# A two-layer decoder trunk: every matrix product with tokens as output rows and 512 weight columns moving, the FFN in two parts, state chunks of 8 tokens, and a program without loops

## What is computed

```python
for i in range(2):
    h = rms_norm(x, norm_mix[i])
    x = x + (gmlp_mixer(h) if i == 0 else s5_mixer(h))
    h = rms_norm(x, norm_ffn[i])
    x = x + (silu(h @ w1[i]) * (h @ w3[i])) @ w2[i]                 # 2048 -> 5632 -> 2048
    gate = sigmoid(rms_norm(x, norm_ple[i]) @ ple_w_gate[i])        # 2048 -> 2048
    x = x + gate * (p[i] @ ple_w_proj[i])                           # 256 -> 2048
return rms_norm(x, norm_final)

# gmlp_mixer: z = gelu(h @ w_in), u, v = split(z); v = layer_norm(v)
#             (u * (tril(w_s) @ v + b_s)) @ w_out, per chunk of 128 tokens and head of 128
# s5_mixer:   u = h @ w_in; 128 groups of 16 channels, 64 complex states each:
#             s[t] = lam_bar * s[t-1] + b_bar @ u[t];  y = Re(c @ s) + d * u
#             val, gate = split(gelu(y) @ w_out);  val * sigmoid(gate)
```

## Time and profile before

| | |
|---|---|
| median of 3 runs | 2567.61 us (2559.71 to 2567.79) |
| span of the profiled execution | 2571.7 us |
| PE busy, and matmul records | 2447.3 us (95%), 14304 |
| DVE, ACT, POOL busy | 1651.7, 1154.5, 329.0 us |
| mean granted clock of PE | 0.971 |
| DMA, mean | 188 GB/s |

### The profile page before, as it was taken

How to read it: one execution, slowest core, us unless ns; L and a number is a source line. 1 busy time by engine, 2 the same in 40 slices (tenths; PEclk the granted TensorE clock), 3 DMA queues, 4 the chain that set the end, 5 groups by cost and what they waited for, 6 DMA issues and landing times.

```text
span 2571.7 us, 39073 instructions
## 1 busy us (share of the span) xinstructions
PE 2447.3 (95%) x14304; PEld 2136.3 (83%) x14304; DVE 1651.7 (64%) x1758; ACT 1154.5 (45%) x1224; POOL 329.0 (13%) x363
## 2 busy tenths in 40 slices
PE   7999798999999999999999999999999999999996
PEld 5887587778878888888889988888888888888885
DVE  7765977767876655555766765666565565555565
ACT  5544244444444444444632224555545555444453
POOL 2001725545552000000000000000000000000000
PEclk9999899999999999999999889999999999999998
DMA  7654376666776665555577865566666666655652
GB/s 239 190 161 134 106 244 194 197 206 181 203 219 205 181 192 188 184 185 177 190 246 218 240 197 165 184 190 184 183 181 194 182 186 186 187 185 185 187 173 99
DMA packets 301371, 484.04 MB, mean 188 GB/s; under 512 B 58800, under 2 KB 85568, under 8 KB 301024
## 3 DMA queue, kind: packets, MB, share of 16 engines
q1 hardware_dynamic: 300224, 479.01, 61.1%
q0 software_dynamic: 848, 3.74, 0.4%
q10 hardware_dynamic: 208, 0.07, 0.0%
HBM read 453.65 MB, written 29.10 MB: 188 GB/s over the span
## 4 chain that ended last, share of the span: by engine, by line
PE 77%; DVE 8%; issue 6%; POOL 5%; ACT 2%; DMA 2%; DVEq 0%; SPq 0%; ACTq 0%; POOLq 0%
PE PS L1570 42%; PE PS L1571 21%; DVE WLO L1052 2%; PE PS L1590 2%; PE PS L1591 2%; PE PS L1592 2%; PE PS L1788 1%; PE PS L1772 1%; PE PS L1663 1%; PE PS L1664 1%; PE PS L1665 1%; PE PS L1786 1%; POOL DTB L703 1%; DMA RAW<-in_s_w_in 1%; POOL DT L704 1%
## 5 line engine op out<-in xcount | busy, mean ns | idle before, releaser
L1052 DVE TENSOR_TENSOR WLO<-RAW,WHI 128x1024 fp32r<-128x1024 f32 x788 | 987.2, 1264 | 822.6 <-ACT WHI L758 818.7
L758 ACT ACTIVATE WHI<-RAW 128x1024 fp32r<-128x1024 f32 x788 | 829.2, 1058 | 1024.6 <-PE PS L1571 871.7
L1570 PE MATMUL PS<-H,WHI 128*128 128x512 f32 x3328 | 1184.1, 401 | 17.4 <-DVE WLO L1052 14.6
L1571 PE MATMUL PS<-H,WLO 128*128 128x256 f32 x3328 | 937.7, 282 | 0.0
L1570 PE MATMUL PS<-M,WHI 128*128 128x512 f32 x2304 | 824.0, 402 | 23.3 <-DVE WLO L1052 21.5
L1570 PEld LDWEIGHTS PS<-H,WHI 128*128 128x128 f32 x3328 | 628.8, 189 | 179.0 <-DVE WLO L1052 21.8
L1571 PE MATMUL PS<-M,WLO 128*128 128x256 f32 x2304 | 652.0, 283 | 0.0
L1571 PEld LDWEIGHTS PS<-H,WLO 128*128 128x128 f32 x3328 | 632.8, 190 | 0.0
L1570 PEld LDWEIGHTS PS<-M,WHI 128*128 128x128 f32 x2304 | 438.0, 190 | 134.3 <-issue 26.7
L1571 PEld LDWEIGHTS PS<-M,WLO 128*128 128x128 f32 x2304 | 440.9, 191 | 0.0
L648 POOL PARTITION_ALL_REDUCE SUM<-SS x7 | 16.1, 2296 | 1585.7 <-DVE SS L1084 1566.8
(11 more groups left out here) (225 smaller groups left out, 1805.9 us busy)
## 6 DMA issues: line engine op xcount, KB each, us to landing
RAW<-in_ffn_w SPq DMA_DIRECT2D x528, 512.0 KB, 3.9
RAW<-in_gm_w_in SPq DMA_DIRECT2D x64, 512.0 KB, 4.1
RAW<-in_ple_w_gate SPq DMA_DIRECT2D x64, 512.0 KB, 4.3
RAW<-in_s_w_out SPq DMA_DIRECT2D x64, 512.0 KB, 4.0
RAW<-in_gm_w_out SPq DMA_DIRECT2D x32, 512.0 KB, 4.1
RAW<-in_s_w_in SPq DMA_DIRECT2D x32, 512.0 KB, 5.3
tabd<-DT SPq DMA_DIRECT2D x16, 512.0 KB, 6.1
tabq<-QS SPq DMA_DIRECT2D x16, 512.0 KB, 4.8
```

Source lines behind the costliest of these rows:

```text
L758: A_.activation(WHI[:, slot, :], RAW[:, slot, :], ACT.Copy).then_inc(hi_ready, 1)
L1052: V_.tensor_tensor(WLO[:, slot, :], RAW[:, slot, :], WHI[:, slot, :].bitcast(F32), ALU.subtract).then_inc(lo_ready, 1)
L1570: T_.matmul(PS[:, QB * s + m, :], WHI[:, slot, w], operand(k), start=(k == 0), stop=False)
L1571: last = T_.matmul(PS[:, QB * s + m, TOK:2 * TOK], WLO[:, slot, w], operand(k)[:, 0:TOK], start=False, stop=(k == TK * depth - 1))
```

## The change

- Every product uses the form of `v`: stationary are 128 tokens by 128 features of the operand, 512 weight columns move, 12 matmuls a tile in one function `tile`. `X` is kept token-major. There are 792 tiles still.
- The next operand must be feature-major, so each finished quarter (4 blocks of 128 features, a quad) is transposed by PE (`turn`, 8 transposes), one or two tiles after the column that made it; ACT and DVE then split it straight out of PSUM (`high`, `low`). There are 50 quads, 4 of them for the input.
- RMS statistics are `bn_stats` along a row on DVE; the reciprocal root is a number for each partition and goes into the activation's scale. `partition_all_reduce`, `cross`, `total` and `scaled` go.
- The FFN runs in two parts (6 and 5 pairs of columns), with the down product of each part after it, so that its operand needs less room.
- S5 chunks are of `T` = 8 tokens, `NC` = 32 chunks. POOL builds all tables, per block: `QT` and `DT` of 512 elements a partition in 12 operations. PE turns `QT` (8 transposes) at `BUILD_A[b]` and makes the taps (9 matmuls) three tiles later, at `BUILD_B[b]`. Tables are kept per group of 16 channels. POOL also makes the rotation tables alone and two of the layer norm's steps.
- The state stage covers 32 tiles of `win` and 24 of `out1` (`EARLY`). Per duo `into_states` has 32 matmuls with 64 stationary columns and 32 moving; `out_of_states` has 16 with 128 by 128 stationary and 32 with 64 rows. u is turned feature-major again (`turn_u`) before it goes through DRAM.
- All hardware loops are written out.

```diff
-STAGES = [
-    ("pro", 1, dict(a=5, q=8, r=4)),
...
+STAGES = [("v", NT, 8), ("us", NT, 8), ("out0", NT, 8),
+          ("up0a", 2 * FA, 8), ("dn0a", NT, 2 * FA), ("up0b", 2 * FB, 8), ("dn0b", NT, 2 * FB), ("gate0", NT, 9),
+          ("win", NT, 8), ("out1", 2 * NT, 8),
+          ("up1a", 2 * FA, 8), ("dn1a", NT, 2 * FA), ("up1b", 2 * FB, 8), ("dn1b", NT, 2 * FB), ("gate1", NT, 9)]
...
+INTO_AT = [W0 + 8 * (d // 2) + 15 + d % 2 for d in range(DUOS)]
+OUT_AT = [W0 + 8 * (d // 2) + 18 + 2 * (d % 2) for d in range(DUOS)]
...
+            def tile(t, dst, block_, first, last_one):
+                slot = t % RING
+                pe.wait_ge(lo_ready, t + 1)
+                for kk in range(TK):
+                    f = slice(NW * kk, NW * kk + NW)
+                    for th in range(2):
+                        hi = OP_of(block_ + kk)[:, P * th:P * th + P]
+                        lo = OP_of(block_ + kk)[:, TOK + P * th:TOK + P * th + P]
+                        begin, finish = first and kk == 0, last_one and kk == TK - 1
+                        T_.matmul(dst[:, th, :], hi, WHI[:, slot, f], start=begin, stop=False)
+                        T_.matmul(dst[:, th, :], hi, WLO[:, slot, f], start=False, stop=False)
+                        last = T_.matmul(dst[:, th, :], lo, WHI[:, slot, f], start=False, stop=finish)
+                last.then_inc(split_used, 1)
...
+                for m in range(QB):
+                    for th in range(2):
+                        src = Z[:, th, P * m:P * m + P] if row is None else X[:, th, NW * i + P * m:NW * i + P * m + P]
+                        at = TOK * (m % 2) + P * th
+                        last = T_.transpose(PS[:, bank + m // 2, at:at + P], src, IDENT[:, :])
...
+            def spread_u(n, h):
+                sp.wait_ge(ud_in, 16 * (n + 1))
...
+                if b:
+                    pool.wait_ge(taps_done, b)
+                    pool.wait_ge(d_out, 16 * b)
```

More of the change, by code:

```diff
@@ L65 @@
 QP = 4
+GB = 8
 DUOS = KB // 2
-STAGES = [
-    ("pro", 1, dict(a=5, q=8, r=4)),
[L73 to L92, removed]
@@ new lines, with start, end, odd_up @@
+ORDER = plan()
+TILES = len(ORDER)
+INDEX = {key: t for t, key in enumerate(ORDER)}
+DEPTH_OF = {name: depth for name, _, depth in STAGES}
+def start(stage, n=0):
+    return INDEX[stage, n, 0]
+def end(stage, n):
+    return INDEX[stage, n, DEPTH_OF[stage] - 1] + 1
+def odd_up(stage, n):
+    return stage[:2] == "up" and n % 2 == 1
+def taken_by_dve(stage, n):
+    return stage[:2] in ("dn",) or stage == "out0" or odd_up(stage, n)
+COLUMNS = sorted(((end(s, n), s, n) for s, cols, _ in STAGES for n in range(cols)))
@@ new lines, with quads @@
+TURN_OF = {key: c for c, key in OWNER.items()}
+QUADS = [("x", n, n, 4 * n, 0, None, 4 + 2 * (n % 2)) for n in range(NT)]
+def quads(stage, cols, block, row, after, per=1):
+    for i, n in enumerate(cols):
+        QUADS.append((stage, n, i, block + 4 * i, row, end(stage, n) + after, 4))
+quads("us", range(NT), 16, None, 1)
+quads("out0", range(NT), 0, 2, 1)
+quads("up0a", range(1, 2 * FA, 2), 16, None, 1)
+quads("up0b", range(1, 2 * FB, 2), 16, None, 1)
+quads("dn0b", range(NT), 0, 4, 1)
+quads("gate0", range(NT), 24, 1, 2)
@@ new lines @@
+RMS = {"v": 0, "us": 0, "up0a": 1, "up0b": 1, "gate0": 2, "win": 3, "up1a": 4, "up1b": 4, "gate1": 5}
+BUILD_A = [start("up0a", 2 * b) + 9 for b in range(FA)] + [start("dn0a", n) + 5 for n in range(NT)]
+BUILD_A += [start("up0b", 2 * b) + 9 for b in range(FB)] + [start("dn0b") + 5]
+BUILD_B = [t + 3 for t in BUILD_A]
+CT_AT = [start("out0") + 12 + 4 * r for r in range(4)]
+MIX_AT = [start("us", n) + 6 for n in range(NT)]
+SET_AT = start("v", 1)
+WT_AT = [start("v", 2) + 2, start("v", 2) + 6]
+PT1_AT = start("up1a") + 5
@@ new lines, in ups @@
+            def ups(stage, pairs, first_block=None):
+                for i in range(pairs):
+                    if i:
+                        quad_of(stage, i - 1, 1)
+                    until(end(stage, 2 * i))
+                    take(stage, 2 * i, in_s, ACT.Silu)
+                    if first_block is not None:
+                        tables(first_block + i)
+                    if stage == "up1a" and i == 0:
+                        until(PT1_AT + 1)
+                quad_of(stage, pairs - 1, 1)
@@ new lines, in downs, with gates @@
+            def downs(stage, i):
+                for n in range(NT):
+                    quad_of(stage, n, 1)
+                until(end(stage, NT - 1) + 4)
+                root(i)
+            def gates(stage, i, last=True):
+                for n in range(NT):
+                    until(end(stage, n))
+                    take(stage, n, in_s, ACT.Sigmoid)
+                    if last:
+                        quad_of(stage, n, 2)
+                if last:
+                    until(end(stage, NT - 1) + 5)
+                    root(i)
@@ new lines, in gates @@
+            def gates(stage, i):
+                for n in range(NT):
+                    until(end(stage, n))
+                    gated(stage, n, PS[:, 6:8, :])
+                    quad_of(stage, n, 2)
+                moments()
+                until(end(stage, NT - 1) + 7)
+                reciprocal(i)
+            ups("up0a", FA)
+            for n in range(NT):
+                add_acc("dn0a", n)
+            ups("up0b", FB)
+            residuals("dn0b", 2)
+            gates("gate0", 3)
```

2260 lines of the change are left out of this document (1051 added, 1209 removed).

## The result

The changed kernel takes 2497.23 us (median of 4 runs, 2493.33 to 2500.09) beside 2567.7 us of the kernel before (4 runs). The ratio is 0.9723, with a 95% interval of [0.969, 0.9755]: 2.8% faster, where 2431 us, 5.3%, was forecast. Direction and time lie inside what was given as a whole (2375 to 2515), but the time lies outside the range of the forecast proper (2385 to 2475); 66 us of the forecast gain are missing.

The account below looks back on a forecast made before the run. PE bounds the kernel. Tiles at 2154 us plus start, turns, tables, state stage, other stages' extras and end sum to a 2435 us span, median 2431, 5.3% less; range 2375 to 2515, the forecast's own 2385 to 2475.

Parts of the forecast that it names:

- The rate: All 792 tiles: 2.72 us each as in `v`, some 15 ns a matmul beside the columns, 2154 us in all.
- A turn: Eight transposes on PE, 0.87 us, plus 0.10 at restart: 0.97 us each, 48.5 us for 50.
- The tables and their turns: Up and down stages with tables: 32 us of PE work for 16 blocks, 5 us of waits for POOL, plus turns.
- Rival C: Stages with tables: POOL late with each block at 3.2 us an operation, 60 us more, 2490 us; chance 0.07.
- Rival E: Whole unrolled program: instruction fetch stalls PE, 145 us at every sixth tile, 2650 at every fourth; chance 0.08.
- list of gains by stages: Gains: 70 and 11 us from rate, 50 tables, 26 `out0`, 7 `us`, 9 start and end; transposes cost 48.5, state stage 4.
- I take 30 us, bounds 10 and 90: State stage: waits and half clock together, beside tiles and small matmuls, put at 30 us.
- Rival B: State stage: DRAM data late, SP's waits holding weight loads, 58 us more waits, some 30 of clock, 2520 us; chance 0.15.
- The prediction's own sign: Wrong if PE waits at turns for DVE, taps for POOL, or states for a DMA over 60 us in all.
- the small matmuls: State stage: matmuls into and out of states, 12.5 us a duo, 100 us in all, bounds 67 and 142.
- `v`: Stage `v`: 12 us beyond its tiles, bounds 6 and 20; the stall on DVE goes, input turns and weight transposes stay.
- `us`: Stage `us`: beyond its tiles 2 us of waits and 10.4 for mixes, 16.3 with 4 turns.

Follow-up runs that it names:

- the last version: Changed kernel with y's DMAs from GpSimd, four bursts, duo 5's y wanted later, start reordered, layer norm's gain and bias on DVE: 2405.53 us, ratio 0.9321.

## Why the prediction was right and where it failed

**Right.** The rate: 2.72 us a tile, in every stage that has nothing else, so some 15 ns beside the columns of each matmul holds for the FFN's tiles as it did for those of `v`. A turn is 0.80 + 0.12 = 0.93 us where 0.97 was taken. The tables and their turns cost 44.9 us for 51.5: 31 of PE's work for 32, and nothing of the 5 us of waits, since POOL is never late. Rival C had POOL's operations too long: the twelve of 512 elements take 1.1 to 2.2 us each, 18.2 a block, where it had 3.2 each and 38. Rival E did not come: 29151 written-out instructions feed PE without a gap in 620 us of FFN. The end is 14.8 us for 17. DVE stays at half in the FFN, 309.55 of 619.8 us, as said. Its list of gains by stages, though, doesn't add up to its own sum: 70 + 11 + 50 + 26 + 7 + 9 less 48.5 and 4 is 121 us of the 137, and the rest was put to `v` and the gates without a figure.

**The step that failed** is "I take 30 us, bounds 10 and 90" for waits and half clock in the state stage. It was 188.6 less 4 turns (3.7) and 76 to 78 of small matmuls, some 107 us, beyond the upper bound. Rival B, at 0.15, named the mechanism: data through DRAM late on an SP queue whose waits hold the weight loads, and the clock falling with the gaps. Its 88 us of waits and 30 of clock, 118, are near the 107, but divided otherwise: 48 idle, 59 of clock. The prediction gave the landing times of u and the distance of one y from its use, and never asked where in SP's order y's DMAs stand. The trace shows u nearly harmless (PE waits 0.8 us for it; the 18.0 at its PSUM copy come behind ACT's wait for y), and y eight times late. The prediction's own sign, PE waiting for more than 60 us at a turn, at the taps or for a DMA, didn't come: the wait for y reaches PE through ACT and DVE, and much of the cost is clock and not wait. What would have shown it before is in the diff: `store_y`, at `OUT_AT` + 9 in SP's list, stands behind the load for tile `OUT_AT` + 9, which waits until DVE has split tile `OUT_AT` + 5, and in five of eight duos behind a table load.

The two causes separate. SP's order is 61 us of the result, 2497.2 - 2435.7, shown by moving y's two DMAs alone. The bursts are worth 12 us as measured, though 90 us at half clock cost 45; the rest is given back by a later y, which the idle time of PE shows (4.1 to 20.7 us). That the forecast would have been near with SP's order mended, 286 for 279, is in part luck: the small matmuls were over-priced, 100 for 78, which hid 22 of the 45 us that half clock still costs there.

**`v`**: 12 us taken, bounds 6 and 20, measured 26.8. The sum had the old start with one stall less, but the statistics of the whole input, which the change puts on DVE, come ahead of a tile's `WLO`; 10 us, shown by the reordered start. **`us`**: 6 us over as a sum, but the term for waits was off by more: 2 us taken, and 22.1 less 4 turns (3.7) and 4 mixes of 1.8 (7.3, for 10.4 forecast) leaves 11. The miss is DVE and POOL working beside each other, shown by the small POOL share, which gains 12, and by the last version. The prediction had DVE's and POOL's steps at their lengths alone.

**Open.** What within a burst drops the clock: how it is cut matters, but its length wasn't told apart from its share of the time around it, nor narrow moving tensors from half-height stationary ones. How late issue and slow landing share the 61 us. And why the state stage varies by 5 us with the same code.

## What to carry to other kernels

Where one engine issues DMAs in a fixed order, the place of a small transfer is a cost of its own: compare when its data are ready with when it is issued, ask which slot the load ahead of it waits for, and look at the size of what is issued just before it. When the waits of the bound engine name an engine with half its time free, follow the wait back engine by engine until it ends at a transfer or at the bound engine itself. In this kernel a long run of small matmuls cost more than its length, since the products behind it ran slow; splitting it helped, and gave part of it back where someone waited for its result.

## What the runs showed of the hardware

- PE's clock fell without any gap. With a burst of 32 records of 128 rows and 64 of 64 rows, at float32 and 32 moving columns, it went to 0.50 about 3 to 4.5 us in and stayed there 10 to 14 us, at every duo of the version with y from GpSimd. The same work in quarters of under 2 us, with half a product tile between them, had a mean of 0.96 over the stage in the run that was profiled.
- DVE beside POOL: the split of 1024 elements took 3.40 us instead of 1.22 and a scaling of 512 elements 8.05 / 4 = 2.0 instead of 1.91 / 4 = 0.48, while POOL ran elementwise steps of 1024 elements from SBUF.
- A 256 KB store took 8.5 to 9.6 us from issue to landing where it was issued right behind a 1 MB load by the same engine (five times), 4.8 to 5.3 where not (three times, same run), and 3.0 as a median where all eight were issued two weight loads earlier.
- A float32 matmul with 64 stationary and 32 moving columns leaves two records, 2.06 / 64 = 0.032 us each, while one of 128 by 128 takes 1.87 / 16 = 0.117 and one with 64 rows 1.98 / 32 = 0.062. With 64 moving columns the 128 by 128 one took 0.108: between 32 and 64 moving columns hardly count here. The smaller forms alternate between the two halves of rows or columns, so whether the size of the block or that alternation makes them shorter isn't shown.
